# GpSimd splits the convolution's weights, and the gathered-row dots get another pace beside the first expert table

## What is computed

```python
# PEER layer: u_table, v_table are (16384, 1024); eidx are 8 x 16 chosen rows per token
ug = jnp.take(u_table, eidx, axis=0)
hid = jnp.einsum('cd,chkd->chk', xc, ug)
a = jax.nn.gelu(hid, approximate=False) * g
out = jnp.einsum('chk,chkd->cd', a, jnp.take(v_table, eidx, axis=0))
...
# second block's convolution: b_cv, c_cv, u_cv are (512, 1024) slices of h @ w_in
u = c_cv * u_cv
conv = u_pad[:, 0:S] * w[0]
for tap in range(1, CONV_K):
    conv = conv + u_pad[:, tap:tap + S] * w[tap]
y_b = (b_cv * conv) @ conv_w_out[l]
```

## Time and profile before

| | |
|---|---|
| median of 3 runs | 2660.97 us (2659.73 to 2661.41) |
| profiled execution | 2654.32 us, span 2652.5 us |
| PE busy | 2512.6 us (95%) |
| DVE busy | 1785.0 us (67%) |
| ACT busy | 1033.4 us (39%) |
| POOL busy | 563.2 us (21%) |
| granted PE clock | 0.982 of full |

### The profile page before, as it was taken

The page is one execution under the profiler, slowest core; times in us unless marked ns, Lnnn a source line. Parts: engine busy times, 40 slices in busy tenths (PEclk is TensorE's granted clock), DMA queues, the critical chain, the costliest instruction groups (busy, mean ns, idle before and its releaser), DMA issues.

```text
span 2652.5 us, 34078 instructions
## 1 busy us (share of the span) xinstructions
PE 2512.6 (95%) x13049; PEld 2221.5 (84%) x13065; DVE 1785.0 (67%) x3405; ACT 1033.4 (39%) x1528; POOL 563.2 (21%) x383
## 2 busy tenths in 40 slices
PE   6999889999999999999999998888999999899998
PEld 4777768889999998999999996777777888788886
DVE  5766457899998998688888876656577334533333
ACT  4444346444555444333333334334322223322221
POOL 4222237022211354233333310322100000000000
PEclk9999899999999999999999999989999999999999
DMA  4111235478887999999999972212266322222231
GB/s 145 68 51 57 80 110 178 159 253 321 300 289 272 342 398 374 344 367 364 369 366 362 371 277 73 80 63 84 68 214 227 99 95 96 80 96 96 96 105 38
DMA packets 190417, 519.06 MB, mean 196 GB/s; under 512 B 15976, under 2 KB 65256, under 8 KB 187056
## 3 DMA queue, kind: packets, MB, share of 16 engines
q1 hardware_dynamic: 153392, 382.66, 40.8%
q0 software_dynamic: 36864, 134.23, 13.9%
HBM read 464.34 MB, written 52.49 MB: 195 GB/s over the span
## 4 chain that ended last, share of the span: by engine, by line
PE 71%; DVE 15%; DMA 6%; issue 3%; ACT 3%; POOL 1%; SPq 0%; DVEq 0%; POOLq 0%; ACTq 0%
PE P L995 22%; PE P L997 21%; PE P L996 21%; DMA GB<-un,SI 4%; DMA AWC<-adat 2%; DVE wl L1415 2%; PE P L1309 1%; DVE T L1415 1%; PE P L1002 1%; DVE GB L1697 1%; DVE RW L1415 1%; DVE RU L1415 1%; DVE T L1418 1%; DVE D L1415 1%; PE P L1242 0%
## 5 line engine op out<-in xcount | busy, mean ns | idle before, releaser
L995 PE MATMUL P<-XH,wh 128*128 128x512 f32 (+1 forms) x2344 | 897.8, 383 | 29.1 <-DVE wl L1415 10.8
L996 PE MATMUL P<-XL,wh 128*128 128x512 f32 (+1 forms) x2344 | 866.0, 369 | 0.0
L997 PE MATMUL P<-XH,wl 128*128 128x512 f32 (+1 forms) x2344 | 866.0, 369 | 0.0
L2031 ACT ACTIVATE wh<-raw 128x1024 fp32r<-128x1024 f32 x467 | 489.4, 1052 | 134.2 <-PE P L997 133.4
L995 PEld LDWEIGHTS P<-XH,wh 128*128 128x128 f32 x2344 | 447.9, 191 | 91.8 <-issue 24.8
L1415 DVE TENSOR_TENSOR wl<-raw,wh 128x1024 fp32r<-128x1024 f32 x388 | 469.4, 1219 | 38.6 <-ACT wh L2031 38.4
L997 PEld LDWEIGHTS P<-XH,wl 128*128 128x128 f32 x2344 | 445.4, 190 | 55.1
L996 PEld LDWEIGHTS P<-XL,wh 128*128 128x128 f32 x2344 | 446.7, 191 | 50.2 <-issue 3.6
L995 PE MATMUL P<-AH,wh 128*128 128x384 f32 x1024 | 342.2, 334 | 0.3 <-issue 0.3
L997 PE MATMUL P<-AH,wl 128*128 128x384 f32 x1024 | 342.0, 334 | 0.0
L996 PE MATMUL P<-AL,wh 128*128 128x384 f32 x1024 | 342.0, 334 | 0.0
(11 more groups left out here) (309 smaller groups left out, 2860.9 us busy)
## 6 DMA issues: line engine op xcount, KB each, us to landing
raw<-wts SPq DMA_DIRECT2D x211, 512.0 KB
raw<-ut SPq DMA_DIRECT2D x128, 512.0 KB
raw<-vt SPq DMA_DIRECT2D x128, 512.0 KB
hdram<-HID SPq DMA_DIRECT2D x64, 384.0 KB
gdram<-GS SPq DMA_DIRECT2D x24, 1024.0 KB, 6.3
GI<-gdram SPq DMA_DIRECT2D x16, 1536.0 KB, 12.2
HI<-hdram SPq DMA_DIRECT2D x32, 768.0 KB
AWC<-adat SPq DMA_DIRECT2D x64, 256.0 KB, 4.7
```

Source lines behind the costliest of these rows:

```text
L995: e.matmul(bank, wh[:, w], H, start=start, stop=False)
L996: e.matmul(bank, wh[:, w], L, start=False, stop=False)
L997: return e.matmul(bank, wl[:, w], H, start=False, stop=stop)
L2031: return e.activation(dst, src, ACT.Copy)
```

## The change

`low_on_pool` now holds for every unit from 307 up to the end of the convolution, so the low parts of the 24 convolution units are made by POOL (L2343) instead of DVE. And the dots due per step n become 1.3, 1.0 and 1.7 in the three stretches n < 30, n < 62 and n >= 62, where they were 1.1, 0.75 and 2.15.

```diff
 def low_on_pool(i):
-    return i < U_U or U_RET + 2 <= i < U_RET + 32
+    return i < U_U or U_RET + 2 <= i < U_GATE
...
-            dots_due += 1.1 if n < 30 else 0.75 if n < 62 else 2.15
+            dots_due += 1.3 if n < 30 else 1.0 if n < 62 else 1.7
             yield from some(int(dots_due))
             dots_due -= int(dots_due)
```

## The result

| | before | after |
|---|---|---|
| median of 20 runs each | 2659.86 us | 2664.51 us |
| lowest to highest | 2656.02 to 2665.18 | 2659.69 to 2668.12 |
| profiled execution (span) | 2654.32 (2652.5) | 2660.86 (2659.1) |

The ratio is 1.0017 with a 95% interval of 1.001 to 1.0023: the changed kernel is slower by 4.6 us. That is inside the forecast range and inside the bound of 0.2%, but the sign is the other one: I had forecast 3 us less. That the time is nearly the 2664 us of rival (c) is luck, since two large terms stand behind it and not one small one. The two profiled executions differ by 6.5 us.

A forecast was written before the change was run, and what follows sets the result against it. PE was taken to bound the kernel, busy 2512.6 of 2652.5 us. Dots -10 and low parts +7.5 gave -2.5, rounded to -3: median 2661 becomes 2658 us, range 2645 to 2669, no change that can be told.

The forecast's parts named there:

- rival (c): Last third of the first table's stage is bound by bytes, 6.1 us loss stays; dots give -4, 2664 us; chance 0.11.
- The dots: First table's stage, last third: 14.1 us lost there, 4 us left in place, so -10 us; ends -14 and 0.
- the wait for GB: Last third of the first table's stage: DVE's wait for gathered rows falls from 18.1 to some 6 us, under 8.
- the ring of four gather buffers: Last third of the first table's stage: every seventh step has three dots, so DVE waits up to 2.7 us for a buffer.
- The low parts: Convolution: POOL's low parts block DVE, 12 us over five phases less 4.4 of slack, +7.5 us; ends -7 and +14.
- the cluster: Convolution: a phase's three `high`s follow CH, so POOL's three low parts fall in a row at the start of the parts.
- the ring of four: Convolution: a load is issued when the part four before is done and lands 4.4 us later, so late parts delay loads.
- My own chain: Convolution: one phase followed part by part from conv's start; part 10 ends at 20.7 us, 19.2 with the shortest landing.
- the rule alone: Convolution: exclusive lock on the port pair, nothing hidden, makes a phase 21.6 us instead of 17.8.
- The slack: Convolution: DVE is 4.4 us ahead of PE at unit 363, taken off the 12 us lost.
- (a): Both halves gain because POOL's low parts fall where DVE waits anyway: -6 and -10, 2645 us; chance 0.25.
- (b): Moved dots find no room in steps 0 to 61: the 10 us are given back, +7.5 stays, 2668 us; chance 0.14.

The follow-up runs named there:

- e8: Kernel before the change with dots due at 1.2, 0.9 and 2.0 a step, never three in a step of the last third: 2655.17 us, ratio 0.9987.
- e1: Kernel before the change with only the dots' new pace, low parts left as before: 2642.35 us, ratio 0.994 against before.
- f3: Dots' new pace alone, low parts as before, plus every hidden tile stored a second time: 2649.6 us, ratio 0.9961 against before.
- f1: Changed kernel with the second input of the 64 AWC instructions in PSUM instead of SBUF: 2637.5 us, ratio 0.9912 against before.

## Why the prediction was right and wrong

**The sum.** Forecast -10 + 7.5; measured alone -16 (-20 to -12 by its interval) and +20 (+16 to +24). Both terms had the right sign, both effects sit in the stretches where I put them, and the result has the wrong sign since the second term was sized at less than half. The first was under-sized too, which hid part of it: that the total missed by no more than 6.5 us (2664.5 for 2658) is luck.

**The dots: right in size by the trace (-12.3 us in the stage), under by the runs, and with a wrong reason.** The rates (4.68 us a unit at clock 1.00), the wait of PE for OM (2.5, forecast under 4), the middle of the stage (4.61, forecast under 4.7) came as written; the wait for GB is 9.7 where I had said 6 to 8. What fell is "What uses it up is the ring of four gather buffers: 2.15 makes every seventh step one of three dots". e8 has no such step and keeps 19.6 us of waits. What e1, e8 and f3 show instead is the load of the stretch. By the count of the forecast, a step needs 1.87 MB in 4.70 us after, 397 GB/s. Before, 1.15 x 0.721 + 2.15 x 0.524 + 0.262 = 2.22 MB in 5.37 us, 413 GB/s; in e8, 1.10 x 0.721 + 2.0 x 0.524 + 0.262 = 2.10 MB in 1.10 x 4.16 + 0.57 = 5.15 us, 408 GB/s. The two schedules that ask for 408 to 413 got 378 to 386 with waits; the one that asks for 397 got 401; and f3, asking for more, got 418 with waits. That last row says that it is not a plain ceiling at 400. The ring is a rival for the rest, since dots and bytes changed together in all but f3: once around the ring, four dots take 4/2.15 x 5.37 = 10.0 us before and 10.3 in e8, but 4/1.7 x 4.70 = 11.1 after, and a gather lands 8.5 to 9.0 us from its issue (e8, after). How the load and the ring of four gather buffers share the loss stays open: a longer ring was not tried. The last window (5.38 us a unit, clock 0.92) kept its loss, as I had feared for rival (c), though by little else of it.

**The low parts: right mechanism, wrong size.** A DVE part that starts 0.22 us into POOL's low part ends 0.5 us after it (2.83 us), the cluster stands behind CH, and the ring of four turns it into late loads: as forecast. The Trainium skill (SBUF — State Buffer, section SBUF: two separate sides) says that of a DVE operation with two SBUF inputs and a GpSimd operation that reads SBUF, the first to start takes the shared port pair for the whole instruction while the other blocks; the trace agrees (2.83 instead of 0.69 us), and f1 shows it from the other side (689 ns on average). The step that failed is "With the shortest landing, 2.8 us, it is 19.2. If the blocks hid every AWC wait (18.5/105 x 17.8 = 3.1 a phase), 18.5. I take 20.2". My own chain had given 20.7 at the usual landing and 21.6 by the rule alone, and I shaded it down by a cover that did not exist: blocks do not hide waits for AWC, on balance they make them (24.5 us instead of 18.5), since a part that ends late issues its successor's load late. The measured 22.5 lies above all of these. In the timeline the chain is ahead of mine up to part 6, which ends 15.0 us behind the start of conv (I had 15.8: a turn costs 2.78 us, 2.61 + 0.17, and I had 3.0), and what puts it behind is the load of part 10: issued 0.3 us after part 6, it takes 6.2 us and not 4.4, so that part 10 ends at 22.1 and not 20.7.

From conv(1) to conv(6) the stage takes 112.7 us instead of 89.1, +23.6 where I had +12. The phase ahead of these is as long as before (18.0 us; I had +1.1), and the last one is 1.2 us shorter, as forecast. The slack was smaller than the 4.4 us that I took: I looked for it at unit 363, and PE stopped at unit 361, whose low part before was ready at 2042.4 for 2045.1, 2.7 us ahead. 23.6 - 0.1 - 1.2 - 2.7 = 19.6 us, against the 19.7 read at unit 361.

**What was missing in the sum.** The slow restart of PE behind the last gap, 1.7 us. The earlier trace rows had shown windows at 0.92 beside the waits at the end of the first table's stage, and I used them for the dots but not for the convolution. The other 8 us or so by which PE was busy longer fell where it would have waited for DVE anyway.

**The rivals.** (a) did not happen, but is what f1 measures: 2637.5 with the lock away. (b) is refuted, 4.61 us a unit in the middle. (c) is refuted for two of three windows, 396 and 403 GB/s. "PE waiting for POOL's wl" and "L2343 x103" came as written.

## What to carry to other kernels

Before elementwise work goes to GpSimd, look for what VectorE does at that moment: if its operations read two SBUF operands, they don't run beside GpSimd but take turns with it, and each of them lasts as long as GpSimd's. Moving one of the two operands to PSUM removes the conflict, and a longer ring of buffers absorbs it. When an engine with a short ring is delayed, price the late loads too: here they made 20 us out of what costs, with two more buffers, 4 us that can't be told from noise. And ask which engine sets the pace before a longer busy time is called a loss: PE was busy 10.1 us longer, and 1.7 us of that were on the path.

## What was not expected of the hardware

- One operand in PSUM frees the DVE instruction from POOL's two-input operation: 689 ns in f1 against 1262 ns on average (2.83 to 2.85 when blocked) in the changed kernel, and POOL's own time falls from 2.6 to 2.40 us.
- The DMA engines carried 418 GB/s over 100 us in f3, where before sustained 386 to 400 at a smaller demand (413 GB/s by the count, against some 440).
- Some small gaps go with a lower clock. Windows from 1940 to 2040 us (all engines), after and then before:

```profile
1940.00:2040.00 100.00, 86.58 (x341) 69.55 (x340) 74.46 (x118) 15.81 (x20) 34.05 (x14) 0.90 0.58 190
```

```profile
1940.00:2040.00 100.00, 94.40 (x412) 76.58 (x411) 76.81 (x159) 22.95 (x30) 0.00 (x0) 1.00 0.67 233
```

PE waits of 2 to 4.4 us, one in some 22 us, stand beside a granted clock of 0.90; waits of up to 1.7 us, one in 18 us, beside 1.00. Behind each of the five waits after, 7 to 13 matmuls start 0.43 us apart instead of 0.23, about 10 us in all. The length of the wait does not decide it alone: one of 2.6 us in e1 had no such matmuls behind it, one of 1.95 us in the changed kernel had.
